# Joining the experts' block and the last stage's block of a decoder kernel

## The reference

```python
def _moe(x, w_group, b_group, w_expert, b_expert, w_gate, w_up, w_down):
    ...   # top-1 group of 4, then the top-2 of its 4 experts; e_w are the two weights
    h = silu(einsum('td,edf->tef', t, w_gate)) * einsum('td,edf->tef', t, w_up)
    h = h * gate[:, :, None]
    return einsum('tef,efd->td', h, w_down)

x = layer_norm(alpha * x + moe(x), ln2_w, ln2_b)
```

## Time and profile before

| | us |
| --- | --- |
| median of three runs | 1511.9 |
| lowest and highest run | 1509.85, 1514.17 |
| profiled execution, its own time | 1513.93 |
| its span in the trace | 1512.3 |
| PE busy in the span | 1368.8 (91%) |
| DVE, ACT, POOL busy | 607.3, 516.7, 368.5 |
| mean granted clock of TensorE | 0.952 |

### The profile page before, as it was taken

One profiled execution on the slowest core, in us unless ns is written; L12 is line 12 of the kernel. 1 busy time (PEld: TensorE's weight loads), 2 busy tenths in 40 slices (PEclk: granted clock), 3 DMA queues, 4 the chain that ended last, 5 costly groups with the idle time before them and its releaser, 6 DMA issues. The chain is left out here.

```text
span 1512.3 us, 23774 instructions
## 1 busy us (share of the span) xinstructions
PE 1368.8 (91%) x8917; PEld 1186.6 (78%) x8917; DVE 607.3 (40%) x1593; ACT 516.7 (34%) x962; POOL 368.5 (24%) x463
## 2 busy tenths in 40 slices
PE   4999999999999999978889978979985999999946
PEld 3999999999888989956565657968875888888822
DVE  6222212222423224044666557863463333333317
ACT  4521222222122221126545555530011343433226
POOL 5311150020202000003333214621033232233207
PEclk9999999999999999979999988989995999999968
DMA  7254394172624224971004018752116878888746
GB/s 210 60 167 146 112 251 119 54 187 63 193 63 147 76 69 69 189 215 33 1 2 161 19 58 249 232 207 84 63 56 176 264 254 279 277 272 285 270 150 254
DMA packets 188964, 228.31 MB, mean 151 GB/s; under 512 B 47607, under 2 KB 157303, under 8 KB 187487
## 3 DMA queue, kind: packets, MB, share of 16 engines
q1 hardware_dynamic: 176270, 186.25, 40.8%
q0 software_dynamic: 12592, 40.71, 8.5%
HBM read 167.89 MB, written 60.19 MB: 151 GB/s over the span
## 5 line engine op out<-in xcount | busy, mean ns | idle before, releaser
L1255 PE MATMUL psum<-proj_x_hi,proj_w_hi 128*128 128x362 f32 (+1 forms) x1056 | 358.2, 339 | 4.1 <-POOL proj_x_lo L1461 2.5
L1255 PE MATMUL psum<-proj_x_lo,proj_w_hi 128*128 128x362 f32 (+1 forms) x1056 | 347.6, 329 | 0.0
L1255 PE MATMUL psum<-proj_x_hi,proj_w_lo 128*128 128x362 f32 (+1 forms) x1056 | 347.4, 329 | 0.0
L1255 PEld LDWEIGHTS psum<-proj_x_hi,proj_w_hi 128*128 128x128 f32 x1056 | 199.9, 189 | 11.5 <-POOL proj_x_lo L1461 4.0
L1255 PEld LDWEIGHTS psum<-proj_x_lo,proj_w_hi 128*128 128x128 f32 x1056 | 200.2, 190 | 0.0
L1255 PEld LDWEIGHTS psum<-proj_x_hi,proj_w_lo 128*128 128x128 f32 x1056 | 199.8, 189 | 0.0
L1380 DVE TENSOR_TENSOR proj_w_lo<-proj_w_raw,proj_w_hi 128x1024 fp32r<-128x1024 f32 x44 | 53.9, 1225 | 271.5 <-ACT proj_w_hi L1288 271.4
L1317 ACT ACTIVATE proj_sig<-psum,proj_bias 128x362 f32<-128x362 f32 (+1 forms) x72 | 40.3, 563 | 240.1 <-PE psum L1255 229.3
L2666 PEld LDWEIGHTS psum<-moe_xgt,expert_gate_w 128*128 128x128 f32 x512 | 85.0, 194 | 13.2 <-issue 13.2
L2666 PE MATMUL psum<-moe_xgt,expert_gate_w 128*128 128x192 f32 x512 | 91.9, 334 | 0.7 <-ACT moe_xgt L2710 0.7
L2666 PE MATMUL psum<-moe_xgt,expert_up_w 128*128 128x192 f32 x512 | 88.5, 327 | 0.0
(11 more groups left out here) (475 smaller groups left out, 2404.2 us busy)
## 6 DMA issues: line engine op xcount, KB each, us to landing
proj_w_raw<-in_w_in SPq DMA_DIRECT2D x43, 512.0 KB, 5.2
expert_gate_w<-in_moe_w_gate SPq DMA_DIRECT2D x16, 1024.0 KB, 6.0
expert_up_w<-in_moe_w_up SPq DMA_DIRECT2D x16, 1024.0 KB, 10.9
expert_down_w<-in_moe_w_down SPq DMA_DIRECT2D x16, 1024.0 KB, 7.6
merge_sig<-gate_scratch SPq DMA_DIRECT2D x24, 544.0 KB, 4.0
gate_scratch<-proj_sig SPq DMA_DIRECT2D x48, 181.0 KB, 2.0
final_pair<-expert_rows SPq DMA_DIRECT2D x8, 1024.0 KB, 11.8
feature_scratch<-proj_feat SPq DMA_DIRECT2D x13, 512.0 KB, 3.0
```

The lines of the kernel that those rows point to most:

```text
L1255: mm = nc.tensor.matmul(k.ps[u % RING][:, 0:w], b[wt][:, x % 2, kk, :], b[xx][:, kk, a0:a0 + w], start=(kk == 0 and i == 0), stop=(kk == K ...
```

## The change

The two blocks become one. `combine_norm` is now `last_programs`, which returns a program for each engine; `experts_and_last` calls them behind the rounds. Between the two, only GpSimd and SyncE are tied: when GpSimd has seen its last stores land it raises `all_stored`, and SyncE fetches rows once it sees that. The fetches go into the six halves of the experts' gate, up and down weight buffers, and the ring of its own goes. The parameter rows are loaded before the wait for `all_stored`. ScalarE makes all diagonals first, then waits for `x1`. `all_rounds` loads `most_tokens` ahead of round 0, and one check for more than 192 tokens stands around the whole loop of further rounds. The bodies of the other programs are the same, indented less.

```diff
-def experts(k, most, ew, ews, idx, x1):
+def last_programs(k, x1, weight, ew, x1_loaded, all_stored):
...
-    st, b, s = phase(k, "final", dict(l2w=[P, D], l2b=[P, D], pair=[P, RB, 2, D], diag=[P, NT, 2, P], ...
+    st, b, s = phase(k, "final", dict(l2w=[P, D], l2b=[P, D], diag=[P, NT, 2, P], ...
+    pair = [ew[n][:, x].rearrange("p k f -> p (k f)") for x in range(2) for n in ("wg", "wu", "wd")]
...
+    def sync(sp):
+        def fetch(t):
+
+            sp.dma_start(pair[t % RB][0:rows(t), :], k.y_dram[0:2 * T, :].rearrange("(t i) d -> t (i d)", i=2)[t * P:t * P + rows(t), :]).then_inc(s[f"rows_loaded{t % RB}"], 16)
+        sp.dma_start(b["l2w"][:, :], io["ln2_w"][0].partition_broadcast(P)).then_inc(s["ln2_par"], 16)
+        sp.dma_start(b["l2b"][:, :], io["ln2_b"][0].partition_broadcast(P)).then_inc(s["ln2_par"], 16)
+        sp.wait_ge(all_stored, 1)
+        for t in range(RB):
+            fetch(t)
...
-            diagonals(0)
-            scaled(0)
-            diagonals(1)
-            scaled(1)
-            for t in range(2, NT):
-                diagonals(t)
+        for t in range(NT):
+            diagonals(t)
+        act.wait_ge(x1_loaded, 16 * NT)
+        scaled(0)
+        scaled(1)
...
     def all_rounds(eng, body):
+        n = eng.value_load(most[0:1, 0:1], min_val=0, max_val=T)
         body(0)
-        n = eng.value_load(most[0:1, 0:1], min_val=0, max_val=T)
-        with eng.Fori(1, ROUNDS) as rnd:
-            with eng.If(n > rnd * CAP):
-                body(rnd)
+        with eng.If(n > CAP):
+            with eng.Fori(1, ROUNDS) as rnd:
+                with eng.If(n > rnd * CAP):
+                    body(rnd)
...
             all_rounds(sp, first_round)
+            last_sync(sp)
             sp.wait_ge(s["x1_loaded"], 16 * NT)
...
             all_rounds(pool, one_round)
+            pool.sem_inc(s["all_stored"], 1)
+            last_gpsimd(pool)
```

More of the change, by code:

```diff
@@ L2544, in experts, with experts_and_last @@
+def experts_and_last(k, most, ew, ews, idx, x1, weight):
     nc, io = k.nc, k.io
@@ L2548, in experts @@
                      ["turned", "xt_copied", "up_mm", "sg_done", "silu_done", "hid_full", "hid_high", "hid_done", "wd_hi_done", "wd_lo_done", "down_mm", "y0_done", "y1_done",
-                      "idx_zeroed", "xg_zeroed", "x1_loaded", "idx_loaded", "idx_copied", "pool_at", "y_stored", "y_free"])
+                      "idx_zeroed", "xg_zeroed", "x1_loaded", "idx_loaded", "idx_copied", "pool_at", "y_stored", "y_free", "all_stored"])
+    last_st, last_sync, last_tensor, last_scalar, last_vector, last_gpsimd = last_programs(k, x1, weight, ew, s["x1_loaded"], s["all_stored"])
     xg = (ew["rows0"], b["xg"])
@@ L2558, in all_rounds @@
     def all_rounds(eng, body):
+        n = eng.value_load(most[0:1, 0:1], min_val=0, max_val=T)
         body(0)
-        n = eng.value_load(most[0:1, 0:1], min_val=0, max_val=T)
-        with eng.Fori(1, ROUNDS) as rnd:
-            with eng.If(n > rnd * CAP):
-                body(rnd)
-    with st, nc.Block() as block:
+        with eng.If(n > CAP):
+            with eng.Fori(1, ROUNDS) as rnd:
+                with eng.If(n > rnd * CAP):
+                    body(rnd)
+    with st, last_st, nc.Block() as block:
         @block.sync
@@ L2703, in _ @@
             all_rounds(pe, one_round)
+            last_tensor(pe)
         @block.scalar
@@ L2745, in _ @@
             all_rounds(act, one_round)
+            last_scalar(act)
         @block.vector
@@ L2914, in build @@
+            last_vector(dve)
 def build(nc, io):
@@ L2965, in build @@
         x1 = left(stack, "x1", [P, NT, D])
-        experts(k, most, ew, ews, idx, x1)
-        combine_norm(k, x1, weight)
+        experts_and_last(k, most, ew, ews, idx, x1, weight)
 INS = ["x_prompt", "x_sample", "cache_nsa", "cache_nsa_win", "cache_fox_kv", "cache_fox_logf", "state_mlstm_c", "state_mlstm_n",
```

223 lines of the change are left out of this document (104 added, 119 removed).

## The result

| | before | after |
|---|---|---|
| median, 15 runs each on one chip | 1514.16 us (1508.95 to 1520.76) | 1509.16 us (1503.09 to 1512.29) |
| ratio, 95% interval | 1 | 0.9964 [0.9952, 0.9977] |
| profiled execution: time / span | 1513.93 / 1512.3 us | 1509.91 / 1508.3 us |

The change is faster, by 5.0 us between the medians (5.4 by the ratio). 8.5 were forecast, and 1504.0 as the time; the measured time lies above the range of 1500.5 to 1507.5. Of the 5.2 us between 1504.0 and 1509.16, 1.7 come from the start: the forecast took 1512.5 for the kernel before, and it came out at 1514.16 here. The other 3.5 are missing gain; in the profiled executions, too, the span fell by only 4.0 us.

A forecast was written before the change was run, and what follows sets the result against it. Waits in a row at the seam bound the kernel, with TensorE pacing the last stage after the first fetch. The sum -8.6 + 0.1 = -8.5 us gave 1504.0 us from about 1512.5, range 1500.5 to 1507.5.

The forecast's parts named there:

- The seam: Between experts and last stage: load, passes, DRAIN and barrier go, first fetch at 1452.2 instead of 1460.8, -8.6 us.
- A: Rival: branches wait for code on the path, or the clock stays low longer; gain only 5 to 6.5 us; chance 0.13.
- B: Rival: GpSimd's signal after its last stores is held until 1460.3 as the DRAIN was; only -0.3 us, about 1512; chance 0.05.
- the DRAIN at the end at 2 us: Sign of being right: the DRAIN closing the last block stays at 2 us, 2099 ns in the kernel before.
- Rival D: The DRAIN moves to the kernel's end and takes 13.7 us; time about as before, 1512 to 1514; chance 0.04.
- The load ahead of round 0: Start of the experts' block: hidden on SyncE and GpSimd, 0.86 us on TensorE, +0.1 us net.
- the wait of 0.75 us: TensorE's wait at 1175.30 for the second expert's gathered rows, taken to cover 0.75 of the load's 0.86 us.
- The clock: TensorE's granted clock at the last stage's start: half speed for 3.8 us as before, no change, bounds -1.9 to +2.1 us.
- The last tile: End of the last stage: what follows its last tile does not depend on when that tile comes; no cost forecast.
- Cover of the parameters, the fetches and ScalarE: Around the seam: parameter loads, six fetches in a row and ScalarE's diagonals cost 0; fetches bounded -0.5 to +1.5 us.

The follow-up runs named there:

- rounds_only: Kernel before, two blocks kept, changed only in all_rounds (count loaded ahead of round 0, one check around further rounds): 1511.25 us, ratio 0.9988.
- seam_only: Changed kernel with the old all_rounds, load of the count and five passes behind round 0 on all engines: 1509.55 us, ratio 0.9976 against the kernel before.

## Why the forecast was too high a gain

- **The seam, right.** First fetch 0.2 to 0.5 us after the landing was expected, 0.29 measured; -8.6 expected, -8.64 measured. Of the rivals, A and B are out: GpSimd's branch took 50 ns, and its signal was not held.
- **The step that failed** is this sentence: "What matters is whether the DRAIN is a cost of the instruction or of the time since the last indirect DMA; both give -8.6 here, since the signal waits for neither." It is true at the signal and false for the kernel. A cost of the instruction that grows with the indirect DMAs since the last DRAIN isn't saved when the DRAIN goes; the next DRAIN pays it. The sum put this return at nothing ("the DRAIN at the end at 2 us" stood among the signs of being right), and that DRAIN took 7504 ns. It ended 5.48 us behind GpSimd's last addition instead of 0.08, so 5.40 us longer, 82 ns for each of the 66 indirect DMAs. The landing of the outputs, 5.45 us behind GpSimd's arrival there, covers that much of the 7504 ns; with what stands behind, the end comes 1.9 us later than before relative to the outputs. Of the 4.5 us between the 8.5 forecast and the 4.0 of the profiled spans this is the largest part. The others are 1.2 at the start, 0.9 in the first tile, 0.3 behind the last and 0.2 from fetch to matmul, and none of these is shown to come from the change.
- **Rival D had the place right and the price wrong.** It asked for 13.7 us, from the reading that something is busy for some 11 us after an indirect DMA, and dismissed it by the same reading ("they are over at 1460, long before"). rounds_only refutes the reading: the same 5452 ns with a start 2.7 us closer to the scatter. The 13679 ns of the earlier trace rows, which made the price, are the wait for a gather's landing, and at the seam all stores had landed. What I should have asked of the earlier trace rows against the earlier trace rows is what the two DRAINs differ in (66 indirect DMAs against none), instead of what their ends had in common.
- **The load ahead of round 0, right in size and covered; what it was set against moved.** TensorE's load and register operations cost 0.87 us to the first turn (0.26 to 1.13), 0.86 expected. The prediction set the wait of 0.75 us against it and said of the gathered rows that they "don't move". They moved: the landing came 17.64 us after the release before and 18.90 after, and TensorE, load and all, still waited 0.95 us for it, not near 0. The second turn waits for this landing in every trace, so the load costs at most what that leaves, and by the medians 0.2 to 0.6 us. The +1.26 of the table is the landing, which came as late as 19.42 and as early as 17.43 in other kernels. One profiled execution can't price such a term.
- **The clock, a term of the range.** Expected: no change, -1.9 to +2.1; measured +0.86 in the first tile. In the five profiles of the new seam with TensorE's load ahead and no dummies the first tile took 6.2 to 6.4 us, in the three without it on TensorE 5.0 to 5.2, and the clock rose 5.4 to 5.8 or 3.1 to 3.4 us after the first matmul. That the load ahead causes it is not shown; I know of no path for it, and the differences of the medians (0.2 to 0.6 us) leave it open.
- **The last tile, +0.33.** Not forecast ("what comes after its last tile does not depend on when that tile comes"). The stretch took 16.67 to 16.69 us in the kernel before and rounds_only, 16.66 in seam_only, and 17.00 or 17.01 in the other eleven. In the slower form GpSimd's last root of the last tile takes 1.52 us, in the other 0.85. rounds_only and seam_only each have one half of the change, so in these two profiles neither half alone brings it. The cause stays open.
- **Cover of the parameters, the fetches and ScalarE: right.** No wait of TensorE after the first tile (24.13 us for the next seven in all traces). Fetch to first matmul took 4.9 us in the two kernels with the old fetches and 4.9 to 5.3 in the twelve with six in a row, inside the bounds that the prediction left. The second parameter row landed at 1436.5 us, not before 1435 as the prediction asked, and nothing waited for it.

The Trainium skill (Runtime: NRT & Kernel Launch, Instruction fetch mechanics) on a taken branch that waits for its code: on TensorE the one branch took 3398 ns, which agrees with it, and was hidden; on GpSimd it took 50 ns, so where the path went no such wait is seen.

## What to carry to other kernels

A barrier that is taken away may leave its price to the next one: follow every instruction of it (each engine's DRAIN above all) to where its work is done instead, and put it against what covers it there. GpSimd's DRAIN after many indirect DMAs is best paid in a stretch where GpSimd waits anyway, by one DRAIN of its own; look for it in the source view of the block's last line, since neither the busy times nor the chain show it. When you count what a DRAIN follows, count in the program and not by the starts of records: two gathers that the program has ahead of a DRAIN start behind it in the trace. Where TensorE must idle ahead of a stage that it bounds, matmuls that nobody reads, just as many as fit before the first data land, keep the clock up; here they were worth about 3 of the 12.6 us gained (2.7 in the profile).

## What the runs showed of the hardware

- GpSimd's DRAIN costs 46 ns behind another, and 78 to 84 ns for each indirect DMA issued since, even where the stores had landed 47 us earlier (the changed kernel's end): 124 ns after 1, 201 to 209 after 2, 364 to 373 after 4, 884 after 10, 5452 to 5587 after 66. Why the 66 cost 5452 ns in the two kernels with two blocks and 5586 or 5587 in those with an early DRAIN is open.
- It also waits for GpSimd's own work. In the last stage, with no indirect DMA since the DRAIN before, it took 2099 to 2108 ns, since it began ahead of the last addition, and ended 0.08 us behind it. Ahead of the experts' block, where a gather was still under way, it took 12.2 to 14.6 us and ended 0.70 us behind the landing, in fourteen traces of fourteen.
- The first tile of the last stage took 1.6 to 2.9 us more than its 3.44 after an idle stretch of TensorE of 12 to 21 us, and the shorter stretch did not make it cheaper (5.40 us after 20.62 us idle, 6.26 after 12.18). With 11.88 us of dummies in that stretch it took 0.07 more (3.51 against 3.44).
- The landing of the same two gathers, issued within 0.3 us of the same time after the release, came up to 2 us apart between executions (17.4 to 19.4 us after it).
